# p_2's projection split around the pool layer, and first halves of two units in fp32, in a three-block transformer kernel

## The reference

```python
h = h + rmsnorm(mixer(rmsnorm(h, mix_pre)), mix_post)       # attention (layer 0), pool_mixer (layer 1)
h = h + rmsnorm(conv_ffn(rmsnorm(h, ffn_pre)), ffn_post)
# pool_mixer: causal means over windows 2, 4, 8, 16 minus the input, one per group of 256 channels,
#   then w_group (256 x 256 per group), times scale
# conv_ffn: (silu(gate) * val) @ w_down, both from conv(h @ w_up), w_up 1024 x 5632
# second block, on the 256 tokens of x:
gate_logits = g_lr @ w_gate_up + b_gate                      # rank 16
h = h + concat(gla, conv) @ w_out ; h = h + swiglu_ffn(rmsnorm(h))
h = h + sigmoid(rmsnorm(h) @ w_ple_gate) * (p_2 @ w_ple_proj)
out = rmsnorm(h, lnf)
```

## Time and profile before

| | |
|---|---|
| median of 3 runs | 904.54 us (901.7 to 905.52) |
| profiled execution | 901.81 us, of which span 899.6 us |
| mean granted TensorE clock | 0.998 |
| busy: TensorE, VectorE, ScalarE, GpSimd | 885.6, 680.8, 502.9, 168.7 us |
| HBM read | 142.82 MB, 160 GB/s over the span |

### The profile page before, as it was taken

How to read it: one execution, slowest core, us unless ns; L and a number is a source line. 1 busy time by engine, 2 the same in 40 slices (tenths; PEclk the granted TensorE clock), 3 DMA queues, 4 the chain that set the end, 5 groups by cost and what they waited for, 6 DMA issues and landing times.

```text
span 899.6 us, 19712 instructions
## 1 busy us (share of the span) xinstructions
PE 885.6 (98%) x7261; PEld 860.6 (96%) x7261; DVE 680.8 (76%) x1178; ACT 502.9 (56%) x848; POOL 168.7 (19%) x160
## 2 busy tenths in 40 slices
PE   9999999999999999999999999999999999999997
PEld 8977889999999998999999999999999999999997
DVE  7768559999994438999999543989888788875556
ACT  6776565666665347666666544554555444444443
POOL 0029530000001025200000003200032333313312
PEclk9999999999999999999999999999999999999999
DMA  7742134545455630355555554343344555564431
GB/s 253 198 127 81 52 138 154 180 180 187 167 212 186 237 146 24 119 187 187 187 183 195 183 211 165 98 184 142 119 163 152 197 189 187 189 232 176 175 141 47
DMA packets 25747, 146.79 MB, mean 163 GB/s; under 512 B 3025, under 2 KB 9185, under 8 KB 10465
## 3 DMA queue, kind: packets, MB, share of 16 engines
q1 hardware_dynamic: 25552, 145.98, 45.7%
q10 hardware_dynamic: 144, 0.13, 0.0%
HBM read 142.82 MB, written 1.05 MB: 160 GB/s over the span
## 4 chain that ended last, share of the span: by engine, by line
PE 92%; DVE 5%; ACT 1%; issue 1%; DMA 1%; POOL 0%; SPq 0%; DVEq 0%; POOLq 0%
PE bank L506 26%; PE bank L507 26%; PE bank L508 26%; PE bank L805 2%; PE bank L1026 1%; PE bank L621 1%; PE bank L821 1%; DVE u_low L1577 1%; PE bank L839 1%; PE bank L636 1%; PE bank L604 1%; PE bank L544 1%; DVE h L1657 1%; PE bank L749 1%; DMA k_heads<-w_dq_dram 1%
## 5 line engine op out<-in xcount | busy, mean ns | idle before, releaser
L506 PE MATMUL bank<-u_high,w_high 128*128 128x256 f32 (+2 forms) x1310 | 374.0, 286 | 0.6 <-issue 0.6
L507 PE MATMUL bank<-u_low,w_high 128*128 128x256 f32 (+2 forms) x1310 | 371.9, 284 | 0.0
L508 PE MATMUL bank<-u_high,w_low 128*128 128x256 f32 (+2 forms) x1310 | 370.6, 283 | 0.0
L1568 DVE TENSOR_TENSOR w_low<-raw,w_high 128x1024 fp32r<-128x1024 f32 (+6 forms) x108 | 186.7, 1729 | 94.4 <-ACT w_high L1142 93.1
L506 PEld LDWEIGHTS bank<-u_high,w_high 128*128 128x128 f32 x1310 | 247.4, 189 | 2.8 <-issue 1.2
L507 PEld LDWEIGHTS bank<-u_low,w_high 128*128 128x128 f32 x1310 | 247.1, 189 | 0.0
L508 PEld LDWEIGHTS bank<-u_high,w_low 128*128 128x128 f32 x1310 | 246.9, 188 | 0.0
L1142 ACT ACTIVATE w_high<-raw 128x1024 fp32r<-128x1024 f32 (+6 forms) x117 | 183.8, 1571 | 66.6 <-PE bank L508 62.3
L506 PE MATMUL bank<-x_high,w_high 128*128 128x256 f32 (+1 forms) x592 | 167.7, 283 | 0.3 <-DVE x_low L2080 0.3
L508 PE MATMUL bank<-x_high,w_low 128*128 128x256 f32 (+1 forms) x592 | 168.0, 284 | 0.0
L507 PE MATMUL bank<-x_low,w_high 128*128 128x256 f32 (+1 forms) x592 | 167.3, 283 | 0.0
(11 more groups left out here) (261 smaller groups left out, 1163.9 us busy)
## 6 DMA issues: line engine op xcount, KB each, us to landing
raw<-w_up_dram SPq DMA_DIRECT2D x66, 1024.0 KB, 4.8
raw<-w_down_dram SPq DMA_DIRECT2D x24, 1408.0 KB, 5.9
raw<-w_gin_c_dram SPq DMA_DIRECT2D x4, 1536.0 KB, 6.3
raw<-w_wo_dram SPq DMA_DIRECT2D x4, 1024.0 KB, 5.0
raw<-w_wout_dram SPq DMA_DIRECT2D x4, 1024.0 KB, 4.7
raw<-w_pgate_dram SPq DMA_DIRECT2D x4, 1024.0 KB, 4.7
raw<-w_gin_v_dram SPq DMA_DIRECT2D x2, 1024.0 KB, 4.8
raw<-w_gin_g_dram SPq DMA_DIRECT2D x2, 1024.0 KB, 4.7
```

Of the source, the lines that this page charges most:

```text
L506: nc.tensor.matmul(out, hi, rhi, start=start, stop=False)
L507: nc.tensor.matmul(out, hi, rlo, start=False, stop=False)
L508: return nc.tensor.matmul(out, lo, rhi, start=False, stop=stop)
L1568: nc.vector.tensor_tensor(wl[n % 2][:, split:cols], raw[n % 2][:, split:cols], wh[n % 2][:, split:cols].bitcast(F32), ALU.subtract).then_i ...
```

## The change

Six edits:

1. `wo`: VectorE's low of the second unit is cut in two (1024 and 512 columns, `second_wo_low`), and each part stands at the end of steps NH + 1 and NH + 2, behind the copies. TensorE takes the first two chunks of that unit when the first part is there.
2. p_2's operands are split in the last `down0` unit (`p_in_parts` on ScalarE, four lows on VectorE in `ffn_down_lows`), into tiles of their own (`p_first_high`, `p_h`, ...) and, for blocks 4 to 7, into `uh` and `ul`.
3. `p_block` 0 and 1 take the place of the fillers around the `fpost0` sums, 2 and 3 that of the eleven, 4 and 5, 6, and 7 stand around the `post1` sums and rows. The banks are 1, 0, 2, 3.
4. Pool: the first four chunks are one fp32 matmul each per token tile, on `h` and on weights times the norm's gain (`pool_weights_in`); the pool unit leaves `pool_share`. Four of the chunks then need no `u_high`, `u_low`. The scaled chunks rotate over three places, the third of them `xf` in SBUF.
5. `f1`: the first four chunks of the first `up1` unit likewise (`half_whole_unit`, `f1_weights_in`); their `u_high` and `u_low`, which the second unit needs, are computed behind the eight chunks. The root goes through ScalarE. `post1`'s scaled chunks rotate over three places as well.
6. Gate: the second matmul reads rows 64 to 79 (`wgu` is loaded twice) and writes a bank of its own.

The diff, cut (the vector code for `post1` is that for `fpost0` with other names; its tail is shown):

```diff
-BY_SQRT = ("a0", "cq", "ck", "a1", "post0", "f0", "fpost0", "post1", "fpost1", "out")
+BY_SQRT = ("a0", "cq", "ck", "a1", "post0", "f0", "fpost0", "post1", "f1", "fpost1", "out")
...
-EMBEDDING_BANKS = (1, 2, 3, 4)
+EMBEDDING_BANKS = (1, 0, 2, 3)
...
+                                                               "pool", "gin_k", "gin_v", "gin_g", "gin_c", "wout",
...
+        p_first_high = sb("p_first_weights_high", [P, DC * P], F32R, stack=pp)
+        p_first_low = sb("p_first_weights_low", [P, DC * P], F32R, stack=pp)
...
+        p_h = sb("p_high", [P, 2, SEQ], F32R, stack=pl)
...
+        pool_weights = flat(pool_sq[:, :, :])
         first_weights, first_u = flat(K[:, :, :]), Q[:, 0:DC, :]
-        p_raw, p_wh, p_wl = flat(p_products[:, :, :]), flat(xh[:, 10:18, :]), flat(xl[:, 10:18, :])
+        p_raw, f1_weights = flat(p_products[:, :, :]), flat(Q[:, 0:DC // 2, :])
+        p_wh = p_first_high[:, :], flat(uh[:, 0:DC // 2, :])[:, 0:DC * P]
+        p_wl = p_first_low[:, :], flat(ul[:, 0:DC // 2, :])[:, 0:DC * P]
...
+                    sp.wait_ge(*done("p block 3"))
                     sp.dma_start(lmask[:, :, :], dram["lmask"]).then_inc(tables_in, 16)
-                    sp.dma_start(wgu[:, :], dram["wgu"]).then_inc(tables_in, 16)
+                    for half in range(2):
+                        sp.dma_start(wgu[64 * half:64 * half + 16, :], dram["wgu"]).then_inc(tables_in, 16)
...
+            def half_whole_unit(n, T, t0):
...
+                for k in range(DC):
+                    if k < DC // 2:
+                        pe.wait_ge(*done(f"f1 h {k}"))
+                    else:
+                        ready[0](k)
+                        ready[1](k)
+                    for b in range(2):
+                        out = bank[BLOCKS[U["first"] + b]["bank"]][:, 0:T]
+                        if k < DC // 2:
+                            tile = slice((k * 2 + b) * P, (k * 2 + b + 1) * P)
+                            nc.tensor.matmul(out, f1_weights[:, tile], h[:, k, t0:t0 + T], start=k == 0, stop=False)
+                            continue
+                        hi, lo = weights(n, k * 2 + b)
+                        last = three(out, hi, lo, uh[:, k, 0:T], ul[:, k, 0:T], False, k == DC - 1)
...
             def keep_busy_whole(n, times):
...
             def keep_busy(n, times):
...
             def spare_products(n, times):
...
             def squares(a, n):
...
+            def p_block(b):
+                if b == 0:
+                    for k in range(2):
+                        pe.wait_ge(*done(f"p weights low {k}"))
+                        pe.wait_ge(*done(f"p low {k}"))
+                if b == 2:
+                    x = BLOCKS[FIRST_BLOCK["down0"] + DC - 1]
+                    pe.wait_ge(freed[x["eng"]], x["freed"])
+                if b in (4, 6):
+                    pe.wait_ge(freed["v"], BLOCKS[through(FIRST_UNIT["pool"]) - 5 + b // 2]["freed"])
...
+                for k in range(2):
+                    half, at = b // 4, (k * DC // 2 + b % 4) * P
+                    last = three(out, p_wh[half][:, at:at + P], p_wl[half][:, at:at + P], p_h[:, k, :], p_l[:, k, :], k == 0, k == 1)
...
             def ffn_up(l, T, sums_name):
...
+                elif l == 1:
+                    half_whole_unit(n0, T, META - HISTORY)
...
-                    keep_busy_early(n0 + DC)
+                    if l == 0:
+                        p_block(0)
+                    else:
+                        keep_busy_early(n0 + DC)
                     last_sums(name, n)
-                    keep_busy(n0 + DC, 4)
+                    if l == 0:
+                        p_block(1)
+                    else:
+                        keep_busy(n0 + DC, 4)
...
+                        if u == 0:
+                            parts_ready(n)
+                        else:
+                            pe.wait_ge(*done("second wo low"))
+                        pe.wait_ge(*done(f"exp {NH - 2 + u}"))
+                    if u == 1 and k == 2:
                         parts_ready(n)
...
-            keep_busy(FIRST_UNIT["pool"], 11)
+            p_block(2)
+            p_block(3)
...
+                    if half == 0:
+                        last = nc.tensor.matmul(out, h[:, c, t0:t0 + nt_], pool_weights[:, at], start=c % 2 == 0, stop=c % 2 == 1)
+                        if c == 3:
...
+                        continue
...
+                if c < DC // 2:
+                    pe.wait_ge(*done(f"a1 h {c}"))
+                    pooled(c, tiles, False)
+                    continue
+                if c == DC // 2:
+                    for i in range(2):
+                        pe.wait_ge(*done(f"p products {i}"))
...
-            p_block(0)
-            p_block(1)
+            p_block(4)
+            p_block(5)
             norm_sums("post1", f"post1 acc {DC - 3}", squares(0, T1), True, late=(DC - 2, DC - 1))
-            p_block(2)
+            p_block(6)
             norm_rows("post1", token_rows(R_BANK, T1))
-            for b in range(3, DC):
-                p_block(b)
-            pe.wait_ge(*done("p products 0"))
-            def p_products_kept(k):
+            p_block(7)
+            def second_unit_ready(k):
...
+                if k < DC // 2:
+                    u_ready("f1")(k)
...
             for pair in range(2):
-                last = nc.tensor.matmul(bank[6][:, pair * SEQ:(pair + 1) * SEQ], wgu[:, pair * P:(pair + 1) * P],
-                                        glr[0:16, :], start=True, stop=True)
+                part = slice(64 * pair, 64 * pair + 16)
+                last = nc.tensor.matmul(bank[6 + pair][:, 0:SEQ], wgu[part, pair * P:(pair + 1) * P], glr[part, :],
+                                        start=True, stop=True)
...
-                    high(n0 + c + 2)
+                    if l > 0:
+                        high(n0 + c + 2)
+                    elif c == DC - 2:
+                        p_in_parts()
+                        pool_weights_in()
+            def p_in_parts():
...
+                for half in range(2):
+                    nc.scalar.activation(by_blocks(p_wh[half]), p_raws[half], ACT.Copy).then_inc(*S.step(f"p weights high {half}"))
...
+                for k in range(2):
+                    nc.scalar.activation(p_h[:, k, :], cv[:, k, 0:SEQ], ACT.Copy).then_inc(*S.step(f"p high {k}"))
+            def f1_weights_in():
...
+            def pool_weights_in():
...
+                for c in range(DC // 2):
+                    cs = slice(c * 256, (c + 1) * 256)
+                    nc.scalar.activation(pool_weights[:, cs], raw[n % 2][:, cs], ACT.Copy, scale=pcol("mix_pre1", c))\
...
+                nc.scalar.activation(wh[n % 2][:, at:2 * at], raw[n % 2][:, at:2 * at], ACT.Copy).then_inc(high_parts, 1)
...
+                if c < DC // 2:
+                    square("a1", c, h[:, c, :], T1, S.step(f"a1 sq {c}"))
+                else:
+                    u_high("a1", c, T1, 0, "mix_pre1")
+                if c in (1, 2):
+                    keep_p_products(c - 1)
+            f1_weights_in()
...
-            keep_p_products(0)
+            keep_p_products(2)
+            T_in, t0 = SEQ + HISTORY, META - HISTORY
...
-                u_high("f1", c, SEQ + HISTORY, META - HISTORY, "ffn_pre1")
-                if c in (2, 4, 6):
-                    keep_p_products(c // 2)
+                if c < DC // 2:
+                    square("f1", c, h[:, c, t0:t0 + T_in], T_in, S.step(f"f1 sq {c}"))
+                else:
+                    u_high("f1", c, T_in, t0, "ffn_pre1")
+                if c == 2:
+                    keep_p_products(3)
+            for c in range(DC // 2):
+                nc.scalar.activation(uh[:, c, 0:T_in], h[:, c, t0:t0 + T_in], ACT.Copy, scale=pcol("ffn_pre1", c))\
+                    .then_inc(*S.step(f"f1 u high {c}"))
+            rms("f1", 3)
...
-                low(n0 + DC)
+                if l > 0:
+                    low(n0 + DC)
+                    return
+                for half in range(2):
+                    dve.wait_ge(*done(f"p weights high {half}"))
+                    nc.vector.tensor_tensor(by_blocks(p_wl[half]), p_raws[half], by_blocks(p_wh[half]).bitcast(F32), ALU.subtract)\
+                        .then_inc(*S.step(f"p weights low {half}"))
+                for k in range(2):
+                    dve.wait_ge(*done(f"p high {k}"))
+                    nc.vector.tensor_tensor(p_l[:, k, :], cv[:, k, 0:SEQ], p_h[:, k, :].bitcast(F32), ALU.subtract)\
+                        .then_inc(*S.step(f"p low {k}"))
...
+            def second_wo_low(half):
+                n = FIRST_UNIT["wo"] + 1
+                cs = slice(0, DC * P) if half == 0 else slice(DC * P, vector_cols(n))
+                dve.wait_ge(high_parts, n + 1)
+                nc.vector.tensor_tensor(wl[n % 2][:, cs], raw[n % 2][:, cs], wh[n % 2][:, cs].bitcast(F32), ALU.subtract)\
...
-                if s == NH + 1:
```

(40 more changed lines are left out.)

128 lines of the change are left out of this document (76 added, 52 removed).

## The result

The kernel after takes **898.08 us** (median of 6 runs, 897.83 to 898.28), the kernel before on the same chip 904.35 us (6 runs, 901.7 to 905.52): ratio 0.9936, 95% interval [0.9919, 0.9953]. The forecast was 900.9 us with a range of 897.5 to 904.1, so the range held the time, and the sign was right. By the bound of 0.5% that the prediction set, the result is "faster", to which it gave 0.32, and not "no change", to which it gave 0.61. The profiled execution went from 901.81 to 898.14 us (3.7), its span from 899.6 to 896.4 (3.2). The sum of the prediction was 3.6. That leaves the question where the median's other 2.6 us come from; experiments 1, 2, 5 and 6 answer most of it.

The account below looks back on a forecast made before the run. TensorE was taken as the bound, busy in 885.6 of the 899.6 us span. Gains of 1.15 + 0.95 + 1.1 + 0.4 = 3.6 us took the median from 904.54 to 900.9 us, range 897.5 to 904.1.

Parts of the forecast that it names:

- 1, wo: Second wo unit: putting VectorE's copies first removes most of TensorE's stop at the transposes; 1.15 us gained (0.5 to 1.7).
- 2, last `down0` unit: Last `down0` unit: the added splitting work on ScalarE and VectorE stays hidden, 2 us of cover left; nothing paid.
- 3, norm and pool start: `fpost0` norm to pool unit: blocks replace fillers, fp32 chunks follow, TensorE sets the pace; 0.95 us gained (0.6 to 1.3).
- 4, first `up1` unit: post1 and first `up1` units: sums 1.7 us earlier, VectorE's longer tail delays the second unit; 1.1 us gained (0.3 to 2.5).
- 5, gate: Gate logits: two matmuls in different row halves take 0.65 instead of 1.06 us; 0.4 us gained (0 to 0.45).
- The base: Whole kernel: savings worked out in the profiled execution of 901.81 us carry over in us to the median of 904.54.
- rival A: wo, pool, `up1`, gate: gaps close altogether, GpSimd holds neither wo half nor new adds; 5.95 us gained, 898.6; chance 0.32.
- Rival C: Where fillers ran: TensorE's granted clock falls from 2.4 to 1.2 GHz during short fp32 bursts; 909 us; chance 0.07.
- B: Second `up1` unit and wo: work moved back on VectorE makes TensorE wait; 1.4 us gained, 903.1; chance 0.15 with D.
- D: Pool and `up1`: TensorE's added fp32 columns and later rows use up VectorE's saving; 903.0 us; chance 0.15 with B.

Follow-up runs that it names:

- kernel 1: The kernel before, unchanged, timed once more: median 903.68 us over 12 runs, ratio to before 1.0007.
- kernel 2: The kernel after with the wo edit undone, both halves of the low ahead of the copies again: 900.5 us, ratio to before 0.997.
- kernel 5: The kernel before with the wo edit alone: 900.54 us, ratio to before 0.9964.
- kernel 6: The kernel before with TensorE's stop filled by twelve spare matmuls ahead of the last head's transposes: 902.62 us, ratio to before 0.9989.
- kernel 4: The kernel after with post1's third scaled chunk in a PSUM bank instead of `xf` in SBUF: 897.71 us, ratio to before 0.9941.
- kernel 10: The kernel after with the first wo half moved behind the low of attention output 6 on VectorE's queue: 897.64 us, ratio to before 0.9935.
- kernel 8: The kernel after with blocks 2 and 3 of p_2's projection cut to one matmul each, left incomplete: 898.17 us, ratio to before 0.9937.
- kernel 9: The kernel after with f1's inverse root by VectorE's nine small operations instead of through ScalarE: 899.45 us, ratio to before 0.9955.
- kernel 3: The kernel after with both gate matmuls on rows 0 to 15 again, one behind the other: 898.46 us, ratio to before 0.9947.
- kernel 7: The kernel after with VectorE's low of the first v unit's weights moved ahead of its copy of the g rows: 898.05 us, ratio to before 0.9937.
- kernel 12: The kernel after with all eight chunks of the first `up1` unit as three-part products, no fp32 half: 900.05 us, ratio to before 0.996.

## Why the prediction was right, and where it was not

**1, wo: right.** 1.15 forecast, 1.02 measured, with the stop of 0.7 where it was put (0.76) and the half held by GpSimd until 99.45 as worked out. The rule of the Trainium skill (GPSIMD Engine Reference, Specifications) held in the trace: the copies from PSUM ran free, the instruction with two SBUF inputs did not. Kernels 4 and 10 show the same by taking the hold away (1.00 to 0.43, 1.83 to 1.22).

**2, last `down0` unit: right.** TensorE has no wait from 331 to 343, and the unit's end is as early as what went before.

**3, norm and pool start: mechanism right, the term mis-sized**, 0.95 forecast and 1.68 measured, over its upper bound of 1.3. Twelve fp32 matmuls took 4.99 us (334.88 to 339.87, 0.416 each) where I took 0.44 from 272 columns: 0.3. And blocks 2 and 3 ended 0.4 us sooner than I had them, at 334.88 against 336.15 less the 0.86 of the earlier start, since the rows came 1.95 us behind the last product (330.83 to 332.78) where I had 2.20, and the blocks 0.59 behind the rows where I had 0.77. The term is also added up wrongly: by its own figures it is 345.49 - 344.4 = 1.1, and the 343.3 given for the eps matmul is 344.4 less 1.15, not 345.6 less 1.15 and 0.95. The mis-sizing is thus 0.6, of which the 24 products gave 0.1 back (3.02 us against 2.9). That blocks 2 and 3 cost 0.1 at most is shown by kernel 8.

**4, first `up1` unit: size right, partly by luck**, 1.1 forecast, 1.2 measured. The forecast had the sums gain 1.7 and VectorE's tail take 0.6 of it back, as a wait of 0.5 to 0.7 ahead of the second unit. In the trace the sums gained 1.1 (366.23 and 369.88, less the 2.52 of the rows), and the second unit had no wait: what it needs from VectorE was ready in time. Two errors of some 0.6 us cancelled. The cover of the second half of that unit's weights was put at 0.3 and is 1.3 (the low ends at 369.44, the first product that reads it starts at 370.75); the third unit's was put at 0.4 and is 0.3. One of the two new adds was held, not both. The parts are larger than their sum suggests: undoing the fp32 half costs 1.6 to 2.0 us (with 0.4 more of hold), undoing the root 1.0 to 1.4. The prediction's sentence that the root keeps the cover is what kernel 9 shows.

**5, gate: wrong.** The forecast was "0.4 gained (0 to 0.45)", with 0 only for the case that the pair doesn't run side by side. It does (0.70 us for the pair, as the Trainium skill's TensorEngine Tiling (Array Packing), Key Properties, has it), and the gain is 0 all the same, because the next unit's weights were not ready. The step that failed is that I priced the instruction and did not look at what its successor waits for. Kernels 3 and 7 show it.

**The base: not foreseen.** Saying "a saving is carried over in us" from 901.81 to the median 904.54 took the spread of before as noise. It was two groups of runs. The forecast from the better group would have been 902.1 - 3.6 = 898.5. As it stands, 900.9 is 2.8 us off, and that the range held the time is luck in part: its lower end came from rival A and a margin for the scatter, not from the sum, and it was a loss of clock that took up the room. Rival C looked for a loss of clock in the changed kernel and wrote, of the kernel before, that "the clock is full in all slices here, through the 1.8 us stop": true of that execution and, by their mean clocks, not of 35 of 59. The loss was in before, and the wo edit took it away, as kernels 2 and 5 show; no run of before itself was traced while it lost its clock. Rule and trace stand thus: the Trainium skill (TensorE: Matmul & The Clock Gate, HAM oscillation) tells of kernels whose waits bring the clock down, and kernel 2's windows agree, with 3.4 us lost behind a wait of 1.87 us; kernel 8's idleness of 0.95 us cost nothing.

**The rivals.** A came nearest in time (898.6) by other means: the gaps did not close altogether, TensorE waits 0.76, 0.37, 0.97 and 0.42 us in them. B is out, since the second unit starts when the sums end, at 367.19, without a wait. D is out, since the places of 3 and 4 gave 1.68 and 1.2 us, and undoing the fp32 half costs 1.6 to 2.0 by kernel 12. C is out for the kernel after: 0.997 or more in all 57 runs of the ten kernels without the stop (two of them at 0.997, with times inside their groups).

**Open.** At equal clock the medians differ by 4.0 us and the profiled spans by 3.2. Of this excess of 0.8, 0.4 lies outside the span (2.2 and 1.8 us), as in kernel 5; which edit takes it away no run shows, since kernel 2, with the wo edit undone, keeps the 1.8. The rest is how the profiled executions lay in their groups: the medians of the spans at full clock are 899.9 and 896.25, and kernel 1's execution, 1.07 us later than that of before at the last transposes (102.46 and 101.39), ends 1.0 later. The 0.38 us lost in the loops of `up1` and `down1` is not assigned to a line. Where the three runs of kernel 6 at 0.996 lost their clock is not known. The fp32 half of the pool unit was not undone by itself, since the second half of the split weights lies in `u_high` and `u_low` there.

## What to carry to other kernels

Read all the times of a kernel with their granted clocks before taking one profile as its state: two groups of times with two clocks are a cost in the kernel, and a saving that removes the cause counts for more than its microseconds in the trace. Price a shortened instruction by what its successor waits for, not by its own duration. When a VectorE instruction with two SBUF inputs stands ahead of something urgent while GpSimd runs, reorder it behind, or move one operand to PSUM.
